# Expert rows gathered feature-major: one-hot products on feature blocks in place of row products, copies and transposes

## The reference, cut to what matters

```python
def hierarchical_moe(h, p):
    ...
    gate = (g_onehot[..., :, None] * (p_top * w_grp)[..., None, :]).reshape(*h.shape[:-1], N_EXPERTS)
    gate = gate.astype(h.dtype)
    y = jnp.zeros_like(h)
    for e in range(N_EXPERTS):
        hid = jax.nn.silu(h @ p["w_e1"][e]) * (h @ p["w_e3"][e])
        y = y + gate[..., e:e + 1] * (hid @ p["w_e2"][e])
    return y
...
    x = x + merged @ p["w_out"]
    x = x + hierarchical_moe(rmsnorm(x, p["g_ffn"]), p)
```

## Time and profile before

| what | us |
|---|---|
| median of 3 runs (635.57 to 635.98) | 635.59 |
| the profiled execution, its own time | 635.66 |
| its span in the trace | 633.8 |
| PE busy | 609.9 |
| DVE busy | 291.0 |
| ACT busy | 186.5 |

### The profile page before, as it was taken

How to read it: one execution, slowest core, us unless ns; L and a number is a source line. 1 busy time by engine, 2 the same in 40 slices (tenths; PEclk the granted TensorE clock), 3 DMA queues, 4 the chain that set the end, 5 groups by cost and what they waited for, 6 DMA issues and landing times.

```text
span 633.8 us, 9981 instructions
## 1 busy us (share of the span) xinstructions
PE 609.9 (96%) x3746; PEld 378.8 (60%) x3746; DVE 291.0 (46%) x813; ACT 186.5 (29%) x582; POOL 149.2 (24%) x341
## 2 busy tenths in 40 slices
PE   8999999999999999999999999999999999978895
PEld 7888867677456667666677767854443444434341
DVE  3343947757883589772043321675133133131302
ACT  5524224532478444423100101121221121112201
POOL 1596727733584525410000000000000000000000
PEclk9999999999899999999999999999999999989999
DMA  9793543222300343322479991099999999999993
GB/s 293 188 292 116 193 166 100 68 67 85 113 2 33 115 152 100 100 67 100 152 224 403 401 394 48 9 400 384 420 420 420 420 419 418 420 421 421 420 412 124
DMA packets 57715, 150.57 MB, mean 238 GB/s; under 512 B 12352, under 2 KB 40448, under 8 KB 45760
## 3 DMA queue, kind: packets, MB, share of 16 engines
q1 hardware_dynamic: 57664, 149.89, 63.2%
HBM read 147.12 MB, written 2.76 MB: 236 GB/s over the span
## 4 chain that ended last, share of the span: by engine, by line
PE 92%; DVE 3%; issue 2%; ACT 2%; DMA 1%; SPq 0%; POOL 0%; DVEq 0%
PE PS L835 28%; PE PS L845 21%; PE PS L1232 10%; PE PS L1126 7%; PE PS L1271 6%; PE PS L1261 5%; PE PS L961 2%; PE PS L918 2%; PE PS L1183 2%; PE PS L986 2%; PE PS L828 1%; PE PS L1028 1%; PE PS L969 1%; PE PS L907 1%; DMA X<-in_x_prompt 1%
## 5 line engine op out<-in xcount | busy, mean ns | idle before, releaser
L835 PE MATMUL PS<-hT,W 128*128 128x320 f32 x416 | 117.2, 436 | 0.0
L835 PEld LDWEIGHTS PS<-hT,W 128*128 128x128 f32 x416 | 77.6, 190 | 33.4 <-issue 3.8
L1232 PE MATMUL PS<-E,xT 128*32 128x256 f32 (+1 forms) x1088 | 62.8, 382 | 8.2 <-issue 7.9
L1232 PEld LDWEIGHTS PS<-E,xT 128*32 128x32 f32 x1088 | 35.9, 110 | 34.8 <-issue 15.4
L2209 POOL TENSOR_SCALAR means<-sums 128x4 f32<-128x4 f32 (+3 forms) x35 | 7.7, 221 | 187.9 <-ACT junk L1371 186.9
L1126 PE MATMUL PS<-h,S 128*128 128x512 f32 (+1 forms) x96 | 48.2, 625 | 0.3 <-DVE S L1999 0.3
L845 PE MATMUL PS<-W,hT 128*128 128x256 f32 (+5 forms) x256 | 41.7, 353 | 0.0
L1271 PE MATMUL PS<-yb,WG 128*128 128x512 f32 (+1 forms) x96 | 38.5, 609 | 0.8 <-DVE yb L2124 0.8
L845 PEld LDWEIGHTS PS<-W,hT 128*128 128x128 f32 (+1 forms) x256 | 31.5, 163 | 8.4 <-issue 1.3
L845 PE MATMUL PS<-W,mergedT 128*128 128x384 f32 (+3 forms) x192 | 35.7, 381 | 0.0
L835 PE MATMUL PS<-uT,W 128*128 128x320 f32 x128 | 34.6, 432 | 0.0
(11 more groups left out here) (316 smaller groups left out, 984.5 us busy)
## 6 DMA issues: line engine op xcount, KB each, us to landing
E<-in_w_e SPq DMA_DIRECT2D x93, 1024.0 KB, 23.0
W<-in_w_in SPq DMA_DIRECT2D x7, 1536.0 KB, 7.1
W<-in_w_in SPq DMA_DIRECT2D x7, 1024.0 KB, 8.1
W<-in_w_mem_kv SPq DMA_DIRECT2D x4, 1024.0 KB, 6.9
W<-in_w_glu SPq DMA_DIRECT2D x4, 768.0 KB, 8.2
W<-in_w_out SPq DMA_DIRECT2D x2, 1536.0 KB, 15.7
X<-in_x_prompt SPq DMA_DIRECT2D x4, 512.0 KB, 4.6
W<-in_w_o_mem SPq DMA_DIRECT2D x1, 1536.0 KB, 6.9
```

Source lines behind the costliest of these rows:

```text
L835: ins = mm(out[:, 0:TOK], w[:, k, cols:cols + 128], rhs[:, k, :], start=(k == 0), stop=(k == kt - 1))
L1232: ins = mm(PS[r:r + B, AB, 128 * which.start:128 * which.stop], xT[:, k, place_ + B * n:place_ + B * n + B], E13[slot][:, which, k, j::2], ...
```

## The change

The rows are gathered feature-major in one step. `normed` now stores `h2` by feature blocks: column block k holds the features 8p + k, so DVE reads `X` and `grow` with a step of 8 elements (32 bytes) and writes densely. `x_products` takes a block of `h2` as the stationary operand and `S` as the moving one, 128 columns, so that the product is already [feature, place]; 8 blocks x 3 tiles = 24 products make a team. They go to bank `ROWS` in two halves of four blocks (for the first team to `ROWS` and `ROWS + 1`), each half is copied to `xT` by ACT. `xg`, its copies and its transposes are gone. In an odd pair PE makes blocks 0 and 1 after `up`, 2 and 3 after `hid_transpose`, 4 to 7 after `down`. The overflow tables are made in two parts later: the first in pair 1, `overflow_teams` in pair 3, both behind `y_copy`; ACT's copy of pair 0's output no longer waits for `ov_ready`. The overflow loop uses the same products.

```diff
-            def tile_rows(banks, t, c):
-                n = TILES[t][1]
-                return mm(PS[:, banks + c, :], S[0:n, t, :], h2[0:n, t, 512 * c:512 * c + 512], start=(t == 0), stop=(t == NT - 1))
-
-            def rows_done(banks, full):
-                for c in range(2):
-                    for t in range(NT):
-                        ins = tile_rows(banks, t, c)
-                    ins.then_inc(full, 1)
-
-            def choose_first(t, c):
+            def x_products(bank_, h, ks, ts):
+
+                for k in ks:
+                    for t in ts:
+                        n = TILES[t][1]
+                        ins = mm(PS[:, bank_, 128 * (k % 4):128 * (k % 4) + 128], h2[0:n, t, 128 * k:128 * k + 128], S[0:n, t, :],
+                                 start=((k, t) == (4 * h, 0)), stop=((k, t) == (4 * h + 3, NT - 1)))
+                return ins
+
+            def x_half(h):
+                return range(4 * h, 4 * h + 4)
+
+            def choose_first(t, h):
                 pe.wait_ge(s["chosen"], t + 1)
-                pe.wait_ge(s["h2_ready"], t + 1 + (c if t == NT - 1 else 0))
-                ins = tile_rows(ROWS, t, c)
+                pe.wait_ge(s["h2_ready"], t + 1 + (h if t == NT - 1 else 0))
+                ins = x_products(ROWS + h, h, x_half(h), (t,))
                 if t == NT - 1:
-                    ins.then_inc(s["rows_full"], 1)
-
-            def choose(g):
-                pe.wait_ge(s["chosen"], g + NT)
-                pe.wait_ge(s["weights_ready"], g)
-                pe.wait_ge(s["y_dve"], 2 * g - 1)
-                pe.wait_ge(s["y_act"], 2 * g - 1)
-                rows_done(ROWS, s["rows_full"])
+                    ins.then_inc(s["xt_full"], 1)
+
+            def choose(g, h, ks):
+                if ks[0] == 0:
+                    pe.wait_ge(s["chosen"], g + NT)
+                    pe.wait_ge(s["weights_ready"], g)
+                elif ks[0] == 4:
+                    pe.wait_ge(s["xt_ready"], 2 * g + 1)
+                ins = x_products(ROWS, h, ks, range(NT))
+                if ks[-1] % 4 == 3:
+                    ins.then_inc(s["xt_full"], 1)
 
...
-            def row_transposes(h, bank_, full):
-
-                for k in range(4):
-                    ins = nc.tensor.transpose(PS[:, bank_, 128 * k:128 * k + 128], xg[:, 4 * h + k::KD], ident)
-                ins.then_inc(full, 1)
-
-            def x_transposes(g, h):
-
-                if h == 0:
-                    pe.wait_ge(s["rows_ready"], 2 * g + 2)
-                elif g > 0:
-                    pe.wait_ge(s["xt_ready"], 2 * g + 1)
-                row_transposes(h, ROWS if g > 0 else ROWS + h, s["xt_full"])
-
...
-            x_transposes(0, 0)
-            x_transposes(0, 1)
...
                 elif p % 2 == 1 and p < PAIRS - 1:
-                    choose(p // 2 + 1)
+                    choose(p // 2 + 1, 0, (0, 1))
                 hid_transpose(p)
                 if p > 0 and p % 2 == 0:
                     add_team(p // 2 - 1, range(3, len(SUMS)))
                 elif p % 2 == 1 and p < PAIRS - 1:
-                    x_transposes(p // 2 + 1, 0)
+                    choose(p // 2 + 1, 0, (2, 3))
                 if p % 2 == 0:
                     spread(p // 2)
                 down(p)
                 if p % 2 == 1 and p < PAIRS - 1:
-                    x_transposes(p // 2 + 1, 1)
+                    choose(p // 2 + 1, 1, x_half(1))
...
-            def row_copies(g):
-                for h in range(2):
-                    act.wait_ge(s["rows_full"], 2 * g + h + 1)
-                    if g > 0 and h == 0:
-                        act.wait_ge(s["xt_full"], 2 * g)
-                    fn(xg[:, 512 * h:512 * h + 512], PS[:, ROWS + h, :], ACT.Copy).then_inc(s["rows_ready"], 1)
-
...
                 act.wait_ge(s["y_mm"], p + 1)
-                if p == 0:
-                    act.wait_ge(s["ov_ready"], 2)
...
-            def normed(t, cols=slice(0, D)):
+            def normed(t, ks=slice(0, KD)):
                 n = TILES[t][1]
-                scaled_rows(h2[0:n, t, cols], X[0:n, t, cols], norm(("f", t)), grow[0:n, cols], s["h2_ready"])
+                src, gain = (x.rearrange("p (q k) -> p k q", k=KD)[:, ks, :] for x in (X[0:n, t, :], grow[0:n, :]))
+                scaled_rows(h2[0:n, t, :].rearrange("p (k q) -> p k q", k=KD)[:, ks, :], src, norm(("f", t)), gain, s["h2_ready"])
 
...
-            st.mark(V_.tensor_tensor(ncmp[:], n_[:, :, None].broadcast_to([128, NE, NJ]),
-                                     const("blocks")[:, None, :].broadcast_to([128, NE, NJ]), ALU.is_gt))
...
+            def overflow_places():
+
+                st.mark(V_.tensor_tensor(ncmp[:], n_[:, :, None].broadcast_to([128, NE, NJ]),
+                                         const("blocks")[:, None, :].broadcast_to([128, NE, NJ]), ALU.is_gt))
...
-                dve.wait_ge(s["rows_full"], 2 * g)
+                dve.wait_ge(s["xt_full"], 2 * g)
...
                 hid_copy(p)
-                if p == 0:
+                y_copy(p)
+                if p == 1:
+                    overflow_places()
+                elif p == 3:
                     overflow_teams()
-                y_copy(p)
```

More of the change, by code:

```diff
@@ L1624, in _ @@
                 elif p < PAIRS - 1:
-                    row_copies(p // 2 + 1)
                     x_copy(p // 2 + 1, 0)
@@ L1635, in _ @@
                 with act.Fori(0, OV_TEAMS) as i:
-                    act.wait_ge(s["ov_rows_full"], 2 * i + 2)
-                    for h in range(2):
-                        fn(xg[:, 512 * h:512 * h + 512], PS[:, ROWS + h, :], ACT.Copy).then_inc(s["ov_rows_ready"], 1)
                     act.wait_ge(s["ov_xt_full"], 2 * i + 2)
@@ L2052, in _ @@
             st.mark(V_.tensor_reduce(rs[:, 8, :], ex4[:, 1], AX.X, ALU.add))
-            normed(2, slice(0, 512))
+            normed(2, slice(0, 4))
             homes(only[2], PS[:, LAST_RANKS, 0:NE])
-            normed(2, slice(512, D))
+            normed(2, slice(4, KD))
             dve.wait_ge(s["logits_exp"], 2)
```

44 lines of the change are left out of this document (21 added, 23 removed).

## The result

| | median us | lowest to highest | executions |
|---|---|---|---|
| kernel before | 634.85 | 633.49 to 636.5 | 20 |
| changed kernel | 636.06 | 634.3 to 638.89 | 20 |

The ratio is 1.0022, 95% interval 1.0012 to 1.0032: the change costs 0.22%, and 1.2 us by the medians. The time lies within the range given, 633.8 to 636.3, but the forecast was a gain of 0.65 us, with 0.10 for a loss of more than 0.2%. That it lies within the range is luck: the range was built on 3 executions with a median of 635.59, and 20 give 634.85. Moved by that difference, it would have been 633.1 to 635.6.

What follows compares the result with a forecast made beforehand. The experts' weight stream was taken to bound the kernel, PE's later savings vanishing in waits. Start -0.75 us, later single transfer 0.1, so -0.65: 635.66 - 0.65 = 635.01, stated as 635.0 us; range 633.8 to 636.3.

Steps and rivals of the forecast that it cites:

- The price of a pass: Gathering in odd pairs: 0.128 us per 128-column product, 6.15 us a team against 7.95; at 0.172, PE's idle time covers it.
- The sum of the waits: PE's waits for the stream, 7.9 + 0.54 us, plus 1.2 lost by one `up`: 1.37 us a team to spare.
- The 0.54 us before the last `down`: PE's wait ahead of the final `down`, taken as waiting for the last weights, which land at 621.6 us.
- the last landing sets the end: End of the experts' stage: PE runs ahead of the weight stream, whose last arrival at 621.6 us fixes the finish.
- The clock rival: Longer wait before pair 14 brings 1.2 GHz: `up` there 1.2 us slower, hidden or some 0.2 us; chance 0.06.
- the start: Pair 0: `up` right behind the seeds, -1.18 us, less three added terms; sum -0.75 us, four transfers that much earlier.
- `normed` with the step: Last tile's first half, ahead of the last `S`: reading two operands with 32-byte steps adds 0.26 us to 0.65.
- The last tile's 16 passes: Start of pair 0: 16 passes take 2.05 us where four took 1.98, adding 0.07 us.
- The tables: Overflow tables made later, in pairs 1 and 3: nothing gained or lost at the end.
- The 0.65 us at the stream's end: Experts' weight stream ends 0.65 us sooner: 0.75 us from pair 0, less 0.1 for a later single transfer.
- the hole: Stream at 287 instead of 420 GB/s from 427 to 433 us, losing 1.90 us; rival that it closes altogether, chance 0.2.
- PE becomes the bound: Rival: above 0.194 us a pass PE sets the end, each 0.01 us more costing 3.4 us; chance 0.08.

Runs made afterwards that it cites:

- The tile order: The changed kernel with each team's 24 products looped tile by tile, blocks inside, instead of block by block; 634.28 us, 1.000 to the kernel before.
- the first four: First four kernels measured together: changed kernel unedited (1.0024), its products tile by tile (1.000), its gathering ahead of `down` (1.0067), its two unused products before pair 13's `down` (1.0009).
- the three variants that leave its start alone: Kernel before with work behind pair 13's `down` (1.0015), with half a microsecond more a team (1.0003), or with unused products in the long waits (1.0005).

## Why the prediction was wrong

*The price of a pass, and the words that its excess would be covered, are the step that failed.* I took 0.128 us from L828, "the same shape". It is the same shape pass after pass; in the changed kernel a 64-row block follows every two of 128 rows, and a pass costs 0.172 (8.26 / 48): 0.112 us for the pass, and 0.19 us for each of the 15 changes of row count or shape in a team. The mean of 0.172 stood in the prediction as the upper bound, from L1183, with the words that a team would cost 0.3 us more "and PE's idle time covers that too". The tile order restores 0.128 (6.33 / 48 is 0.132) and with it the time of the kernel before, so this step was both mis-sized and decisive. The price was to be had from the trace of before: its row products change from 128 to 64 rows too, and the ends of their passes of 512 columns lie 0.429 us apart at equal row counts, 0.624 and 0.627 at a change. The Trainium skill, TensorE: Matmul & The Clock Gate, LDWEIGHTS, says that a weight load's time goes by its columns and that 32 rows take as long as 128. The load records agree (192 and 185 ns), yet the pass does not follow from that: what a change of row count costs is an interval between passes, and not a longer load. Why the chip takes it, no run here shows.

*The sum of the waits was taken as slack.* From 7.9 + 0.54 + 1.2 us I made 1.37 us a team and a threshold of 0.194 us a pass, below which PE would not be the bound. Slack ahead of the last long wait is of no use behind it. Behind `down` of pair 13 there were 1.26 + 0.92 = 2.18 us, and the change put 4.23 us where 0.64 stood. The overrun, 3.59 - 2.18 = 1.4 us, could be read from the diff and the rows: with 0.128 a pass it would have been 3.07 - 0.64 - 2.18 = 0.25. The work placed there in the kernel before (3.6 us, 1.0015) and half a microsecond a team elsewhere (1.0003) bear this out, though the two intervals overlap. So does the path from the end of `down` of pair 13 to the last `down`: it takes 22.61 us in both traces of the changed kernel, with no wait for the stream in it, and 21.36 in before with 2.18 us of such waits.

*The 0.54 us before the last `down` was misread.* I called it a wait for the last landing. It is there in every kernel, also in those in which PE waits for nothing else, and in the changed kernel, where nothing of the stream arrives any more in the 1.7 us before. In the run with the extra products before `down` of pair 13 the chain gives this time to DVE's copy of `hid`:

```profile
619.28 0.30 DVE hidT L2098
```

It is no slack, and "the last landing sets the end" was not shown by it; PE's last real wait was the 0.92 us before pair 15. The clock rival counted 0.92 + 0.54 = 1.46 us to spare, of which 0.92 was real.

*The clock rival (a slow spell behind a wait) was right in kind and wrong in place.* I looked for the slow spell in `up` of pair 14; in both traces of the changed kernel it came in `down` of pair 13, and in the first cost 1.73 us with no slack behind it. Its chance of 0.06 stood for "some tenths later" beside a 0.65 us gain. The Trainium skill's rule (TensorE: Matmul & The Clock Gate, HAM oscillation) lets long waits bring the slow clock back. The tile-by-tile run agrees (waits of 3.68, 4.04 and 2.61 us, and a slow piece behind each). The run with gathering ahead of `down` does not: there the fall came in passes of 128 columns with 0.67 us of waiting before them. Nor does a spell cost much while there is slack: the tile-by-tile kernel has the lowest clocks of the first four but that one (0.992 or less in all 12 executions) and the shortest median.

*Right in the main:* the start. `up` stands straight behind the seeds, `normed` with the step takes 1.04 us where the sum had 0.65 + 0.26, and the four transfers come 0.54 us earlier against 0.75. The last tile's 16 passes are the worst of its terms, 2.27 us against 2.05. The tables have no part in the time, and the stream keeps its rate.

*The 0.65 us at the stream's end, the only gain in the sum, is in no run shown.* The last three transfers are issued 185.57 to 186.11 us after the first six in before and the three variants that leave its start alone, mean 185.81; in the eight traces with the earlier start it is 184.75 to 186.27, mean 185.45. The difference of 0.36 is less than the spread of either. The 1.90 us of the hole were read from one execution; at 380 GB/s for the 14 us, as in those variants, it is 14 x (1 - 380/420) = 1.3. The tile-by-tile kernel has the early start and the cheap pass, and its ratio of 1.000 leaves room for 1 us either way.

So of the rivals "PE becomes the bound" came true, at 0.172 us a pass and not above 0.194, since only the last three pairs had to run out of slack. The changed kernel, without an edit and with the tables back, has medians of 636.0 to 636.3; undoing any one of three things gives 634.3 to 635.0: the price of a pass, the place of the last team's passes, the slow spell at pair 13. For the first of the three this is shown; for the other two the medians say so and the intervals (to 1.0024 and 1.0026) leave both answers open. That the loss needs all three together fits the medians and is not shown. How the 1.2 us divide among them stays open too.

## What to carry to other kernels

Slack is what an engine still waits behind the last long wait, not the sum of its waits: before moving work past a transfer's landing, add up the waits that are left from there to the end. When small matmuls are priced by a row of the same shape, check that they also stand in the same sequence, and price the changes of row count apart: here a pass costs 0.112 us and a change 0.19, so ordering a loop by shape made 24 passes 3.07 us in place of 4.23. A rate read from one execution (287 GB/s in the hole) should be looked up in a second before a gain is built on it. A wait is known as a wait for a transfer only if its length differs between kernels or places; one that is the same 0.54 us everywhere belongs to something else.

## What was not expected of the hardware

- Between fp32 passes, a change of the weights' row count from 128 to 64 or back costs 0.19 us: ends 0.303 to 0.307 us apart instead of 0.112 with 128 columns, 0.624 to 0.627 instead of 0.429 with 512. Entering 128-column weights from 32-column ones (`up` or `down` into the gathering) costs the same, 0.307. In a team that makes 0.172 us a pass alternating and 0.132 sorted.
- Weights of products read with a step of 32 bytes: the load goes from 192 to 332 ns, the pass to 0.311 us at either level of the granted clock, and PE's clock fell to 1.2 GHz in each gathering without a wait. The transposes of the kernel before load their data with the same step in 194 instead of 140 ns, for 0.71 instead of 0.66 us per four. Why products pay so much more than transposes is not shown.
- DVE with a step of 32 bytes on two operands: 1131 against 736 ns for 512 elements and 2094 against 1282 for 1024, 0.8 us per 1024 elements. The Trainium skill, Advanced Engine Details and Errata, Memory Cachelines, names the penalty without a price; both engines' rows agree with it, and the weights of TensorE's products pay the most.
- Each stretch at 1.2 GHz that followed a wait in the experts' stage cost a busy PE up to 1.7 us (`down` in 3.58 instead of 1.85 us, `up` in 5.4 instead of 3.8).
